# Rounded products first, low products last: the order of 48 matmuls inside a weight tile

## The reference

```
u = rms_norm(h, g_norm) @ w_in          # HGRN2 mixer: 64 column tiles of 128
...
h + (o * silu(z)) @ w_out               # 16 tiles
u = rms_norm(h, g_kv) @ w_kv            # shared keys, values, forget gate: 33 tiles
u = rms_norm(h, g_norm) @ w_in          # attention q and z: 32 tiles, then w_out: 16
proj = xn @ w_in + b_in                 # second block: conv 16 tiles, k, v, q 10, w_out 16
qh = xt @ peer_w_q                      # router queries: 16 tiles
h = einsum("cd,chkd->chk", xc, u_sel)   # experts, "up": computed for all 16384 experts, 128 tiles
y = einsum("chk,chkd->cd", gelu(h) * gate, v_sel)   # "down": 128 tiles
```

## Time and profile before

| | us |
|---|---|
| median of 3 runs | 3547.64 (3545.72 to 3549.3) |
| the profiled execution's own time | 3545.76 |
| its span, first to last instruction | 3543.9 |
| TensorE busy | 3275.0 (92%) |
| VectorE busy | 2021.0 (57%) |
| ScalarE busy | 1694.6 (48%) |
| GpSimd busy | 763.9 (22%) |
| mean granted TensorE clock | 0.931 of full speed |

### The profile page before, as it was taken

One profiled execution on the slowest core, in us unless ns is written; L12 is line 12 of the kernel. 1 busy time (PEld: TensorE's weight loads), 2 busy tenths in 40 slices (PEclk: granted clock), 3 DMA queues, 4 the chain that ended last, 5 costly groups with the idle time before them and its releaser, 6 DMA issues.

```text
span 3543.9 us, 66107 instructions
## 1 busy us (share of the span) xinstructions
PE 3275.0 (92%) x25842; PEld 3210.5 (91%) x25842; DVE 2021.0 (57%) x3416; ACT 1694.6 (48%) x2641; POOL 763.9 (22%) x329
## 2 busy tenths in 40 slices
PE   7999989999999855769769999999999999999999
PEld 7999989999998855659669999999999999999999
DVE  4555546544445799566996555554445555554444
ACT  5666655666775433664212344444442244444443
POOL 3333324444343665314530000000000000000000
PEclk9999989999999987869877799999998799999999
DMA  5343334444333422214321155555553145555553
GB/s 190 140 142 137 135 107 160 165 168 152 140 132 122 174 89 83 72 50 176 119 89 61 70 187 189 180 179 186 178 185 112 60 155 189 179 181 185 179 185 134
DMA packets 72271, 506.35 MB, mean 143 GB/s; under 512 B 7904, under 2 KB 10592, under 8 KB 11232
## 3 DMA queue, kind: packets, MB, share of 16 engines
q1 hardware_dynamic: 71584, 503.09, 40.2%
q10 hardware_dynamic: 576, 1.72, 0.1%
HBM read 502.69 MB, written 2.10 MB: 142 GB/s over the span
## 4 chain that ended last, share of the span: by engine, by line
PE 83%; DVE 9%; issue 4%; ACT 3%; DMA 0%; DVEq 0%; SPq 0%; ACTq 0%
PE bank L422 11%; PE bank L424 10%; PE bank L423 10%; PE bank L1741 7%; PE bank L1743 7%; PE bank L1742 7%; PE bank L1917 7%; PE bank L1916 7%; PE bank L1915 7%; PE bank L1730 5%; DVE c_acc L1163 2%; PE bank L625 1%; DVE r_oh L1591 0%; ACT c_pr L1377 0%; PE bank L640 0%
## 5 line engine op out<-in xcount | busy, mean ns | idle before, releaser
L399 ACT ACTIVATE whi<-raw 128x1024 fp32r<-128x1024 f32 x950 | 998.0, 1057 | 1259.5 <-PE bank L424 518.4
L406 DVE TENSOR_TENSOR wlo<-raw,whi 128x1024 fp32r<-128x1024 f32 x682 | 823.7, 1223 | 393.9 <-ACT whi L399 393.7
L406 POOL TENSOR_TENSOR wlo<-raw,whi 128x1024 fp32r<-128x1024 f32 x268 | 710.9, 2657 | 1071.0 <-ACT whi L399 1065.4
L422 PE MATMUL bank<-xa_hi,whi 128*128 128x272 f32 (+1 forms) x2064 | 608.1, 295 | 3.5 <-DVE xa_lo L1398 3.0
L424 PE MATMUL bank<-xa_hi,wlo 128*128 128x272 f32 (+1 forms) x2064 | 599.5, 290 | 0.0
L423 PE MATMUL bank<-xa_lo,whi 128*128 128x272 f32 (+1 forms) x2064 | 597.8, 290 | 0.0
L1741 PE MATMUL bank<-xb_hi,whi 128*128 128x256 f32 x2048 | 590.0, 288 | 1.1 <-DVE hT L1962 1.1
L1742 PE MATMUL bank<-xb_lo,whi 128*128 128x256 f32 x2048 | 589.6, 288 | 0.0
L1743 PE MATMUL bank<-xb_hi,wlo 128*128 128x256 f32 x2048 | 588.5, 287 | 0.0
L1916 PE MATMUL bank<-e_coef_lo,whi 128*128 128x256 f32 x2048 | 579.6, 283 | 0.0
L1915 PE MATMUL bank<-e_coef_hi,whi 128*128 128x256 f32 x2048 | 579.6, 283 | 0.0
(11 more groups left out here) (381 smaller groups left out, 4748.5 us busy)
## 6 DMA issues: line engine op xcount, KB each, us to landing
raw<-in_w SPq DMA_DIRECT2D x219, 1024.0 KB, 4.8
raw<-in_u SPq DMA_DIRECT2D x128, 1024.0 KB, 4.8
raw<-in_v SPq DMA_DIRECT2D x128, 1024.0 KB, 5.3
hT<-in_hT SPq DMA_DIRECT2D x4, 544.0 KB, 8.3
out<-hT SPq DMA_DIRECT2D x8, 256.0 KB, 2.7
r_keys<-in_keys ACTq DMA_DIRECT2D x1, 1024.0 KB, 4.8
c_mask<-in_masks ACTq DMA_DIRECT2D x1, 320.0 KB, 2.9
params<-in_params SPq DMA_DIRECT2D x1, 238.5 KB, 2.6
```

The costliest lines, as they stand in the source:

```text
L399: act.activation(whi[:, (2 * t.q + half) % 4, :], raw[:, t.q, half * 1024:(half + 1) * 1024], ACT.Copy).then_inc(w_hi_done, 1)
L406: eng.tensor_tensor(wlo[:, slot, :], raw[:, t.q, half * 1024:(half + 1) * 1024], whi[:, slot, :].bitcast(F32), ALU.subtract).then_inc(w_lo ...
L422: te.matmul(ps, hi, x[0][:, kk, cols], start=(kk == 0), stop=False)
```

## The change

In the projections and the up tiles TensorE runs the 32 products with `whi` first, both halves, and then the 16 products with `wlo`. Before each half of the first part it waits for `w_hi_done`, before each half of the second part for `w_lo_done`. `halves_done` is raised after the low products of a half. Down tiles are as before.

```
@@ project
             for half in range(2):
-                te.wait_ge(w_lo_done[half], t.n + 1)
+                te.wait_ge(w_hi_done, 2 * t.n + half + 1)
...
                 slot = (2 * t.q + half) % 4
                 for k in range(8):
                     kk = half * 8 + k
-                    hi, lo = whi[:, slot, k * P:(k + 1) * P], wlo[:, slot, k * P:(k + 1) * P]
+                    hi = whi[:, slot, k * P:(k + 1) * P]
                     te.matmul(ps, hi, x[0][:, kk, cols], start=(kk == 0), stop=False)
                     te.matmul(ps, hi, x[1][:, kk, cols], start=False, stop=False)
-                    last = te.matmul(ps, lo, x[0][:, kk, cols], start=False, stop=(kk == KT - 1))
+            for half in range(2):
+                te.wait_ge(w_lo_done[half], t.n + 1)
+                slot = (2 * t.q + half) % 4
+                for k in range(8):
+                    kk = half * 8 + k
+                    last = te.matmul(ps, wlo[:, slot, k * P:(k + 1) * P], x[0][:, kk, cols], start=False,
+                                     stop=(kk == KT - 1))
                 last.then_inc(halves_done, 1)
```

More of the change, by code:

```diff
@@ L1735, in up_project @@
             for half in range(2):
+                te.wait_ge(w_hi_done, 2 * t.n + half + 1)
+                slot = (2 * t.q + half) % 4
+                for k in range(8):
+                    kk = half * 8 + k
+                    hi = whi[:, slot, k * P:(k + 1) * P]
+                    te.matmul(ps, hi, xb[0][:, kk, 0:SEQ], start=(kk == 0), stop=False)
+                    te.matmul(ps, hi, xb[1][:, kk, 0:SEQ], start=False, stop=False)
+            for half in range(2):
                 te.wait_ge(w_lo_done[half], t.n + 1)
@@ L1739, in up_project @@
                     kk = half * 8 + k
[L1740 to L1743, removed]
+                    last = te.matmul(ps, wlo[:, slot, k * P:(k + 1) * P], xb[0][:, kk, 0:SEQ], start=False,
+                                     stop=(kk == KT - 1))
                 last.then_inc(halves_done, 1)
```

## The result

The changed kernel takes 3558.47 us (median of 12 runs, 3554.17 to 3560.27) against 3547.18 for the kernel before (12 runs, 3543.85 to 3549.3): ratio 1.0030, 95% interval 1.0021 to 1.0039. That is slower by more than the 0.2% that can be told from no change. The profiled execution took 3559.62 us, with a span of 3557.8 us in place of 3543.9. The forecast was 3552.0 in a range of 3542 to 3559. The range holds the median by 0.5 us, and so only just; the point is 6.5 us low, and "no difference" had been given twice the chance of "slower".

The account below looks back on a forecast made before the run. TensorE was taken to set the pace of some stages and VectorE of others, such as conv and router. Terms -0.6 + 0 + 0 + 5 = +4.4 us on 3545.76 gave 3550.2, or 3552.0 against the median; range 3542 to 3559.

Parts of the forecast that it names:

- The second tile: First mixer: the kernel's second tile no longer waits for VectorE's `wlo` and starts earlier, -0.6 us.
- the sign: Router stage: six heads take 23 to 23.6 us each in place of 22.33.
- Two signs: Router stage: `r_cand` takes 0.77 us in every head, and `r_cij` takes over 2.
- The overlay: Router stage: GpSimd's new times laid over VectorE's old ones; stalls of 5.9 us a head after, 4.6 before.
- The tile in the sliding-window stage: Sliding-window stage: a tile waiting 2.44 us for GpSimd's `wlo` starts earlier but wins nothing, since VectorE sets the time: 0.
- the router's upper end: Router stage: six heads lose 1.3 us more each and the seventh 1.7 more, 9.5 us; +5 was taken.
- the second block: Router stage: GpSimd's second closed pair in a head, from +11.8 to +16.6 us; its place was called not sure.
- The lower end: Router stage: the stalls only change places, 4.6 us a head as before: 0, or down to -3.
- rival A: Router's heads: blocks cost the full 9.5 us, and TensorE's new step is not free either; 3556.5 us, chance 0.19.
- The new neighbour of two products: TensorE, 347 tiles: low-part product followed by the next block's rounded one; 1.6 ns either side, 8.9 us, taken as 0.
- a block costs the same wherever it stands: Conv stage: GpSimd's blocks move by up to 0.9 us at no cost: 0, within 2.4 us either way.

Follow-up runs that it names:

- e1: Changed kernel, but the 16 router tiles keep the old product order: 3550.23 us, ratio 1.0013.
- e6: Changed kernel, with GpSimd's low parts in the router stage held until VectorE has begun a choice of 16: 3537.34 us, ratio 0.9970.
- e8: Changed kernel, with the release of `whi` split from that of `wlo` by a semaphore of its own, raised earlier: 3546.76 us, ratio 0.9996.
- e2: Kernel before, with the new product order in the 16 router tiles alone: 3556.91 us, ratio 1.0031.
- e4: Kernel before, with the new product order in the up tiles alone: 3549.75 us, ratio 1.0010.
- e5: Kernel before, with GpSimd's low parts in the router stage held until VectorE has begun a choice of 16: 3529.18 us, ratio 0.9949.
- e10: Kernel before, with GpSimd's router low parts held for VectorE's choices of 16 and the up tiles' products as three runs of 16: 3525.49 us, ratio 0.9937.
- e3: Kernel before in its old product order, with `halves_done` raised late for the first half, after the 39th product: 3557.77 us, ratio 1.0030.
- e7: Changed kernel, with the up tiles' 48 products as three runs of 16: 3553.02 us, ratio 1.0017.
- e9: Changed kernel, with `whi` released separately and earlier, and GpSimd's router low parts held for VectorE's choices of 16: 3527.75 us, ratio 0.9941.
- e11: Kernel before, router low parts held for choices of 16; three product runs in up, down and projections outside conv, sliding window and router: 3520.14 us, ratio 0.9920.

## Why the prediction came out as it did

**What held.** The place and the mechanism. The second tile starts 6.13 us behind the first (29.04 to 35.17) where it was 6.72: -0.59, predicted -0.56. The up window has 751 matmuls, as predicted. The roundings stand back to back, GpSimd's operations come as closed pairs, and six heads take 23.47 each, within the 23 to 23.6 named as the sign. Two signs held in part: `r_cand` is free in seven of eight heads, and `r_cij` takes over 2 us in one; in most others the operation next to it is the one held up. The overlay's stalls, 4.6 us a head before and 5.9 after, come out at 4.3 and 5.8. The tile in the sliding-window stage that waited 2.44 us for `wlo` starts without that wait, at 1402.67, and the stage is not shorter: the early tile was worth nothing.

**The term that was sized too low: how much of the router's upper end to take.** The overlay gave at most +9.5 for the stage. Over the stage the heads cost 6 x 1.14 + 2.13 = +9.0 us; 1.1 of it came back by the granted clock in the stage's first tile, as shown above, and +7.8 is left. The prediction took +5, "near the middle of 0 and 9.5", for doubt about where the second block falls. The lower end, that the stalls only change places, had no row for it: it was not worked out, only allowed. Taking the overlay at its own value would have given 3556.5, rival A's figure, 2.0 under the measured median. Rival A's condition, a head longer by 1.3 us, was met nearly (1.14).

This term is the smaller part of the miss. In the profiled execution the forecast was +4.4 and the measurement +13.9: of the 9.5 us between them the router has 2.8, the up stages 3.2, the conv and sliding-window stages 2.1, the output projection behind them 0.7, and the first mixer 0.7, since the 0.6 us won at its second tile don't show in its length. So that rival A comes within 2 us is in part luck: its 9.5 us for the router stage are 1.7 more than the stage lost, and it has nothing for the others.

**The term put at nothing that wasn't quite.** The new neighbour of two products: bounded at 1.6 ns, taken at 0. The up tiles' median step moves by 0.19 ns, 1.2 us over both segments. In the 272-wide tiles of the first mixer it moves the other way, 127.94 to 127.30; the stages' lengths there don't follow it (-0.5 and +0.6), with the granted clock at 0.95 in the first of them where it was 0.96. The shared keys' stage, 272 wide too, does follow: 212.72 us in the changed kernel and in e1, e6 and e8, and 213.50 or 213.51 in the kernel before and in e2, e4, e5 and e10, which have the old order there; e3, e7 and e9 are longer than both (214.2 to 215.0), with a lower granted clock at the stage's start. So the new neighbour costs a little in one kind of tile and gains a little in another, and the length of the whole shows neither. e8 has the same neighbours and lies between 0.13% faster and 0.05% (1.8 us) slower than before; its earlier release has a part in that (-0.6 us in the router stage), so it bounds order and release together.

**The conv and sliding-window stages: 0 predicted, within 2.4; +2.1 measured.** Near the edge of what was allowed, and the reason given, that a block costs the same wherever it stands, failed in one place. The conv stage's loss sits in its first round, between the first two `c_ar`. Before, and with the change:

```profile
1212.09 0.42 DVE L1200 TENSOR_TENSOR c_ar<-bank,rinv 128x256 f32<-128x256 f32 x1 [4.63 <-PE bank L424]
...
1238.34 0.41 DVE L1200 TENSOR_TENSOR c_ar<-bank,rinv 128x256 f32<-128x256 f32 x1
```

```profile
1212.21 0.42 DVE L1206 TENSOR_TENSOR c_ar<-bank,rinv 128x256 f32<-128x256 f32 x1 [4.63 <-PE bank L429]
...
1239.85 0.41 DVE L1206 TENSOR_TENSOR c_ar<-bank,rinv 128x256 f32<-128x256 f32 x1
```

That is 26.25 us and 27.64, and in this round VectorE's operations are held up for 1.4 us longer (12.3 and 13.7); in the later rounds they are held up for 11.7 to 11.9 us each in both kernels. All five with the late raise there (the changed kernel, e1, e3, e6, e7) have 27.5 to 27.7, and all six with the old raise (the kernel before, e2, e4, e5, e10, e11) 26.2 or 26.3. e7's stage is still 0.2 us shorter than before, because its first `c_ar` comes 6.1 us into the stage and not 7.6. With the early release e8 has 26.4, but e9, the same there, 27.3; that isn't explained. The sliding-window stage has about +1 in the changed kernel, e1, e3 and e6, but +1.2 in e5 as well, which changes nothing there: what that loss goes with is open.

## What to carry to other kernels

An order of work on one engine is also an order of releases: before reordering, list what each semaphore raised inside the block frees and how early it could be raised, and where one semaphore frees two buffers, split it (e8). If laying one engine's new times over another's old ones gives a price, take that price unless a row speaks for a lower one. And where two engines shut each other out, let the one that can wait run under the other's operations that are not held up: that was worth 3.65 us a head here (22.33 to 18.68) and 0.5% of the kernel.

## What the runs showed of the hardware

- Small operations are held up for as long as large ones. `r_cij` on 128x32 numbers takes 2.37 us where its twin takes 0.17, and the conversion to `r_topf` (128x64) takes 0.18 in the head shown and 2.40 in e6, where GpSimd's second operation met this one instead (the last fence). In the changed kernel the conversion takes 2.33 to 2.40 in four heads. Each of the two operations has a single input. The Trainium skill (SBUF — State Buffer, section Who interferes with whom; the words that the prediction quotes stand in the same page's section Summary: rules for kernel authors) counts cast and tensor_scalar among the operations that can take both port pairs, and tensor_reduce among those that never contend on trn2. The trace agrees with both: `TENSOR_REDUCE` at 1730.65 keeps its 0.69 us in the middle of a GpSimd block.
- The choices of 16 keep their times under GpSimd's blocks: `FIND_INDEX8` takes 0.42 us at 1720.75, ahead of the block, and 0.42 at 1723.26, inside it. Each choice of the head is thus a cover of 4.2 us (1719.89 to 1724.07 here), and one of a tile's scores of about 3; the 7 us in the expectation of e5 is too long for either.
- The pace of TensorE at the full clock depends a little on the order of products with the same operands: in the up tiles a median step of 118.32 ns in the old order, 118.51 in the new, and in three runs 117.45 to 117.53 in four stages and 118.34 to 118.36 in two; in the 272-wide tiles of the first mixer 127.94 in the old order and 127.30 in the new.

VectorE in e6, the conversion held up:

```profile
1734.38 0.45 DVE L1592 TENSOR_SCALAR r_cij<-r_ci 128x32 uint32<-128x32 uint32 x1
...
1734.83 2.40 DVE L1594 CAST r_topf<-r_topi 128x64 f32<-128x64 uint32 x1
```
